# Interleaving the attention and mLSTM cores with the weight slabs of their projections

## The chip, the cores and the metric

The kernel runs on one core of one Trainium2 chip. The metric is device time in microseconds of one execution. The engines are called as in the profile: PE (TensorE, matmuls), PEld (its weight loads), DVE (VectorE), ACT (ScalarE), POOL (GpSimd), SP (the queue that issues the weight DMAs). Each engine works through its own list of instructions in order; between engines only semaphores order the work.

## What is computed

The reference runs two transformer blocks over 256 positions of width 1024: one with two FFNs and a gated delta mixer, then one with a differential attention layer, an MLP, an mLSTM layer and a second MLP. The change touches the attention and the mLSTM layer:

```
# attention: 8 heads, q and k of 2 x 64, v of 128
q, k, v = split(h @ w_in, 3)                   # w_in: 1024 x 3072
logits = q.k * 64**-0.5 + bias;  p = softmax(logits, causal)
attn = p[:, 0] - lam * p[:, 1]
o = rmsnorm(attn @ v, subln) * (1 - lambda_init);  out = o @ w_out
# mLSTM: 4 heads, q and k of 128, v of 256
q, k = silu(causal conv4((h @ w_in)[qk]));  v, o_pre = the next columns
Sc = (q.k) * exp(D - m);  num = Sc @ v;  den = sum(Sc)
h = num / max(|den|, exp(-m));  out = (sigmoid(o_pre) * rmsnorm(h)) @ w_out
```

## The kernel before

All activations are kept transposed (features on the partitions, 256 positions along the row). Every weight matrix is cut into slabs of 1024 x 256, and `Plan` lists the slabs in the order in which they are used. SP loads them into four `raw` buffers. To keep float32 accuracy with fast matmuls each slab is split into a high part `w_hi` and a low part `w_lo`, in two halves of four row tiles. ACT casts both halves (`split_hi`, L1021), DVE subtracts for half 0 (`ahead`, L1469) and POOL for half 1 (L549). There are four half buffers, so a half can be split once the half four places earlier has been multiplied. `half` on PE (L591) is 24 matmuls of 128x128 on 256 columns: high by high, high by low, low by high. On ACT and DVE, `ahead(n)` prepares slab n+1 while PE works on slab n.

A projection of w columns is a row of slabs into PSUM banks 0 and 1 in turn. When both halves of a slab are multiplied (`filled`), ACT evicts the bank (`evict`, L1087).

Attention (`attention`, one function for each engine) runs 12 slabs `aqkv` (four of q, four of k, four of v) one after another, then turns v by transposes (L880), and only then works off the heads: `scores` on PE (L891), bias, scaling and row maxima on DVE (L1924 to L1930), four exponentials on ACT (L1362), the combination of the two softmaxes on DVE (L1939 to L1947, signalled as `a_comb`), three transposes of it on PE (L904), a copy (L1371), the product with v on PE (L909 to L911) and a copy (L1373). After the last head one normalisation over all eight heads follows (L1951 to L1957), 16 transposes (L916), and the four slabs `ao` of the output projection.

mLSTM runs the gate matmuls (L926), four slabs `mqk` with a convolution on DVE (L1995, L1996) and a SiLU on ACT, eight slabs `mvo` (v and the output gate), and then four heads: row broadcasts and scores on PE (L950 to L953), exponentials on ACT (L1421), weighted scores on DVE (L2012), the products (L966 to L970), sums of squares (L974), root, reciprocal and scaling (L1432, L2027, L2028), gating (L2032) and the split of the result. Then the four slabs `mo`.

The order on each engine is written out by hand; nothing is planned at run time. On PE a wait holds back everything behind it.

## Time and profile before

| | us |
|---|---|
| median of 3 runs | 1689.58 (1689.15 to 1689.95) |
| profiled execution, its own time | 1690.33 |
| its span, first to last instruction | 1688.5 |
| PE busy | 1524.3 (90%) |
| DVE, ACT, POOL busy | 828.6, 690.7, 508.6 |
| mean granted TensorE clock | 0.948 of 2.4 GHz |

PE is busy 90% of the span, so the idle tenth and the stretches at the lower clock are what a reordering can reach. The shares are averages over stages; the two stages of the change lie from about 969 to 1120 us (attention) and from 1321 to 1484 us (mLSTM).

### The profile page before, as it was taken

Reading aid. Unit: us, or ns where it says so; the run is one execution under the profiler, and the core shown is the slowest. Engines: PE = TensorE matmul, PEld = TensorE weight load, DVE = VectorE, ACT = ScalarE, POOL = GpSimd, SP = SyncE. Lnnn points to the kernel's source line nnn. Section 1 sums busy time; section 2 is a strip of 40 time slices with the busy share of each in tenths; the row PEclk is TensorE's granted clock in tenths of the full one; section 3 lists DMA queues with packets and bytes.
Section 4 is the critical chain, followed back from the end, with each engine's and each line's share of the span. In section 5 each row is a group of like instructions: output and inputs, shape, how many; then the busy total and the mean of one; then the engine's idle time right before and its main releaser. Section 6 shows DMA issues by size and latency. Waiting matters only on the chain.

```text
span 1688.5 us, 30721 instructions
## 1 busy us (share of the span) xinstructions
PE 1524.3 (90%) x13577; PEld 1421.7 (84%) x13577; DVE 828.6 (49%) x1133; ACT 690.7 (41%) x961; POOL 508.6 (30%) x209
## 2 busy tenths in 40 slices
PE   5799999797987899899999898699999798899998
PEld 2699998686877787889999797589999597789997
DVE  0432335768676645673334533664433543754333
ACT  1343434543424442444444244535533355445432
POOL 0334432221112211334344242034444141234442
PEclk8899999898988999999999999699999898899999
DMA  9667683732212433336656363046565243245551
GB/s 325 172 219 256 197 277 118 256 104 72 77 51 76 153 123 127 125 125 225 225 169 203 115 200 125 1 137 188 175 200 175 72 154 101 73 127 187 189 185 39
DMA packets 236356, 258.31 MB, mean 153 GB/s; under 512 B 8442, under 2 KB 215744, under 8 KB 236224
## 3 DMA queue, kind: packets, MB, share of 16 engines
q1 hardware_dynamic: 229968, 252.13, 45.5%
q10 hardware_dynamic: 6255, 4.22, 1.3%
q8 instruction: 107, 1.75, 0.4%
q14 instruction: 26, 0.21, 0.0%
HBM read 253.71 MB, written 2.62 MB: 152 GB/s over the span
## 4 chain that ended last, share of the span: by engine, by line
PE 77%; DVE 12%; DMA 4%; ACT 4%; issue 3%; POOL 0%; SPq 0%; DVEq 0%; ACTq 0%
PE ps L591 63%; PE ps L799 4%; DMA bias_rows<-brow 2%; PE ps L565 2%; PE ps L615 2%; DVE w_lo L1469 1%; DVE uf L1501 1%; DVE rstd L1506 1%; DMA raw<-in_w_ada 1%; DVE mt L1604 1%; PE ps L574 1%; ACT w_hi L1021 1%; PE ps L863 1%; PE ps L849 1%; PE ps L926 1%
## 5 line engine op out<-in xcount | busy, mean ns | idle before, releaser
L591 PE MATMUL ps<-u_hl,w_hi 128*128 128x256 f32 x4544 | 849.2, 289 | 43.3 <-DVE w_lo L1469 16.6
L549 POOL TENSOR_TENSOR w_lo<-raw,w_hi 128x1024 fp32r<-128x1024 f32 (+1 forms) x204 | 508.1, 2492 | 1158.0 <-ACT w_hi L1021 1158.0
L591 PEld LDWEIGHTS ps<-u_hl,w_hi 128*128 128x128 f32 x4544 | 724.9, 196 | 66.8 <-issue 53.8
L591 PE MATMUL ps<-u_hl,w_lo 128*128 128x256 f32 x2272 | 651.0, 287 | 0.0
L1021 ACT CAST w_hi<-raw 128x1024 fp32r<-128x1024 f32 (+1 forms) x408 | 410.4, 1038 | 216.4 <-PE ps L591 198.3
L1469 DVE TENSOR_TENSOR w_lo<-raw,w_hi 128x1024 fp32r<-128x1024 f32 x204 | 310.0, 1522 | 317.8 <-ACT w_hi L1021 317.2
L591 PEld LDWEIGHTS ps<-u_hl,w_lo 128*128 128x128 f32 x2272 | 444.9, 196 | 0.0
L591 PE MATMUL ps<-mid_hi,w_hi 128*128 128x256 f32 x864 | 244.8, 283 | 0.0
L591 PE MATMUL ps<-mid_hi,w_lo 128*128 128x256 f32 x864 | 243.1, 281 | 0.0
L591 PE MATMUL ps<-mid_lo,w_hi 128*128 128x256 f32 x864 | 243.1, 281 | 0.0
L591 PEld LDWEIGHTS ps<-mid_hi,w_hi 128*128 128x128 f32 x864 | 162.7, 188 | 1.0 <-issue 0.8
L591 PEld LDWEIGHTS ps<-mid_lo,w_hi 128*128 128x128 f32 x864 | 162.7, 188 | 0.2
L591 PEld LDWEIGHTS ps<-mid_hi,w_lo 128*128 128x128 f32 x864 | 162.6, 188 | 0.0
L1885 DVE TENSOR_TENSOR mt<-sil 128x512 f32<-128x512 f32 x32 | 22.2, 693 | 92.6 <-ACT sil L1335 92.6
L565 PE MATMUL ps<-raw,cpad 128*32 128x512 f32 x288 | 40.2, 676 | 18.7 <-ACT cpad L1111 9.9
L1076 ACT CAST mid_hi<-mt 128x512 fp32r<-128x512 f32 x22 | 13.6, 619 | 96.8 <-DVE mt L1556 84.1
L1335 ACT ACTIVATE sil<-ps 128x512 f32<-128x512 f32 x32 | 19.2, 599 | 82.3 <-PE ps L591 82.3
L615 PE MATMUL ps<-uf,cst 128*128 128x256 f32 x144 | 40.3, 412 | 9.3 <-DVE uf L1484 9.3
L1556 DVE TENSOR_TENSOR mt<-sil,ps 128x512 f32<-128x512 f32 x22 | 15.1, 688 | 67.3 <-PE ps L591 67.3
L1534 DVE TENSOR_TENSOR hT<-hT,ps 128x512 f32<-128x512 f32 x16 | 11.0, 688 | 67.0 <-PE ps L591 67.0
L615 PEld LDWEIGHTS ps<-uf,cst 128*128 128x128 f32 x144 | 27.1, 204 | 17.6 <-DVE uf L1484 13.1
L1069 ACT ACTIVATE sil<-ps 128x512 f32<-128x512 f32 x22 | 13.2, 598 | 67.8 <-PE ps L591 67.8
(320 smaller groups left out, 1361.7 us busy)
## 6 DMA issues: line engine op xcount, KB each, us to landing
raw<-in_mlp_w SPq DMA_DIRECT2D x64, 1024.0 KB, 5.2
raw<-in_w_ffn_up SPq DMA_DIRECT2D x44, 1024.0 KB, 5.1
raw<-in_w_ada SPq DMA_DIRECT2D x36, 1024.0 KB, 5.5
raw<-in_w_in SPq DMA_DIRECT2D x30, 1024.0 KB, 5.1
raw<-in_w_ffn_down SPq DMA_DIRECT2D x16, 1024.0 KB, 6.0
raw<-in_attn_w_in SPq DMA_DIRECT2D x12, 1024.0 KB, 4.9
raw<-in_mlstm_w_in SPq DMA_DIRECT2D x12, 1024.0 KB, 5.1
raw<-in_w_ffn_down SPq DMA_DIRECT2D x8, 768.0 KB, 4.5
```

The lines of the kernel that those rows point to most:

```text
L549: pool.tensor_tensor(w_lo[half][:, 0:k, :], src, w_hi[half][:, 0:k, :].bitcast(F32), ALU.subtract).then_inc(low_ready(n, h)[0], 1)
L565: mm = pe.matmul(bank(b)[32 * k:32 * k + 32, :], cpad[:, 4 * a + k, :], raw4[r][:, k, :], start=(a == 0), stop=(a == 1), skip_group_check= ...
L574: mm = pe.matmul(bank(b)[:, q:q + 1], row_at(p)[:, q * P:(q + 1) * P], cs("ones")[:, 0:1], start=True, stop=True, skip_group_check=True)
L591: mm = pe.matmul(bank(b)[:, m * S:(m + 1) * S], a, c[:, k0 + kt, :], start=(first and m == 0 and kt == ks.start and q == 0), stop=(last an ...
L615: mm = pe.matmul(bank(2)[:, 0:S], cs("ones"), uf[:, k, :], start=(k == 0), stop=(k == KD - 1))
L799: mm = pe.matmul(bank(b)[rows, o:o + CH], left[rows, n, h, :], right(rows, n, h), start=True, stop=True)
L849: mm = pe.matmul(bank(4)[rows, h * P:(h + 1) * P], bmat[rows, n, h, :], rr[rows, h, :], start=True, stop=True)
L863: mm = pe.matmul(bank(5)[rows, h * P:(h + 1) * P], attm[rows, n, h, :], vn[rows, h, :], start=True, stop=True)
L1021: act.copy(w_hi[t % HALVES][:, 0:k, :], src).then_inc(hi_ready, 1)
L1335: act.activation(r, two(b), ACT.Relu).then_inc(bank_free[b], 1)
L1469: dve.tensor_tensor(w_lo[half][:, 0:k, :], src, w_hi[half][:, 0:k, :].bitcast(F32), sub)\
L1885: link(dve.tensor_tensor(m, r, r, mul))
```

## The change

The columns of q, k and v are no longer three blocks. The slabs come as q, k, v of heads 0 and 1, then of heads 2 and 3, and so on (four rounds j = 0 to 3 of three slabs, six halves called slots 0 to 5). During round j the heads 2j-2 and 2j-1 are worked off between the halves. The last two heads fall between the halves of the output projection, which is cut into two halves of its rows (heads 0 to 3, heads 4 to 7), with the normalisation in three parts (four, two and two heads). In mLSTM the q and k slabs come as 0, 2, 1, 3, and the four heads run between the halves of the eight `mvo` slabs. The first heads' results are kept in new buffers `x_hi`, `x_lo`, and several buffers of mLSTM are doubled. The matmuls of the projections and the work of each head stay as they were, but for small copies (`emb` on ACT) and smaller pieces of the normalisation.

```diff
-    columns("aqkv", A["attn_w_in_2"][0], 12)
-    columns("ao", A["attn_w_out_2"][0], 4)
+    for j in range(4):
+        for part in range(3):
+            plan.weight(("aqkv", 4 * part + j), A["attn_w_in_2"][0], 0, 8, (4 * part + j) * SLAB)
+            plan.group("aqkv", 4 * part + j)
+    for kh in range(2):
+        for c in range(2):
+            plan.weight(("ao", kh, c), A["attn_w_out_2"][0], 4 * kh, 4, 2 * c * SLAB, True)
...
+MQK = (0, 2, 1, 3)
@@ PE, attention @@
-                columns("aqkv", 12, U, u_ready("attn"))
...
-                for h in range(8):
-                    if h + 2 < 8:
-                        scores(h + 2)
                     pe.wait_ge(s("a_comb"), h + 1)
...
+                for j in range(4):
+                    for part in range(3):
+                        key = ("aqkv", 4 * part + j)
+                        b = open_bank(*key)
+                        for h in range(2):
+                            half(plan.slab[key], h, b, U, h == 0, h == 1, first if j == 0 and part == 0 else None)
+                            slot = 2 * part + h
+                            if j and slot == 1:
+                                v_columns(j - 1)
+                            if j and slot == 2:
+                                turn(2 * j - 2)
+                            if j and slot == 3:
+                                products(2 * j - 2)
+                                turn(2 * j - 1)
+                            if j and slot == 4:
+                                products(2 * j - 1)
+                            if j == 3 and slot == 4:
+                                pe.wait_ge(s("a_sread"), 5)
+                                features(0, 2)
+                                features(1, 3)
+                    scores(2 * j)
+                    scores(2 * j + 1)
...
+                pe.wait_ge(s("a_ready"), 2)
+                out_half(0, 0, X, every, True, False)
+                v_columns(3)
+                out_half(0, 1, X, every, True, False)
+                turn(6)
+                pe.wait_ge(s("a_sread"), 7)
+                out_half(0, 2, X, every, True, False)
+                products(6)
+                turn(7)
+                pe.wait_ge(s("a_sread"), 8)
+                features(2, 4)
+                out_half(0, 3, X, every, True, False)
+                products(7)
+                pe.wait_ge(s("a_ready"), 3)
+                for g in range(4):
+                    out_half(1, g, U, (0, 1), False, False)
+                    if g == 2:
+                        features(3, 5)
+                pe.wait_ge(s("a_ready"), 4)
+                for g in range(4):
+                    out_half(1, g, U, (2, 3), False, True)
+                    if g:
+                        squares("mlp0", g - 1)
+                squares("mlp0", 3)
@@ ACT, attention @@
+                for j in range(4):
+                    ahead(plan.slab[("aqkv", j)])
+                    if j == 3:
+                        root(0)
+                    if j:
+                        exps(2 * j - 2)
+                    take(0, j)
+                    ahead(plan.slab[("aqkv", 4 + j)])
+                    if j:
+                        v_columns(j - 1)
+                        exps(2 * j - 1)
+                        turned(2 * j - 2)
+                    take(1, j)
+                    ahead(plan.slab[("aqkv", 8 + j)])
+                    if j:
+                        outputs(2 * j - 2)
+                        turned(2 * j - 1)
+                        outputs(2 * j - 1)
...
+                    take(2, j)
@@ DVE, attention @@
+                for j in range(4):
+                    if j:
+                        scores(2 * j - 2)
+                    if j == 3:
+                        normed(0)
+                    ahead(plan.slab[("aqkv", j)])
...
+                    if j:
+                        scores(2 * j - 1)
+                    ahead(plan.slab[("aqkv", 4 + j)])
+                    if j:
+                        combined(2 * j - 2)
+                    ahead(plan.slab[("aqkv", 8 + j)])
+                    if j:
+                        combined(2 * j - 1)
+                    if j == 2:
+                        squared(0)
...
+                ahead(plan.slab[("ao", 1, 0)])
+                low(3, u_lo[:, 6:8, :], u_hi[:, 6:8, :])
+                ahead(plan.slab[("ao", 1, 1)])
+                for g in range(4):
+                    dve.wait_ge(halves_done, 2 * plan.slab[("ao", 1, g // 2)] + g % 2 + 1)
...
@@ PE, mLSTM @@
+                for j in range(8):
...
+                    half(n, 0, b, U, True, False)
+                    if j == 0:
+                        start_columns()
+                    if 1 <= j <= 4:
+                        v_columns(j - 1)
+                    if j in (2, 3):
+                        sums(j - 2)
+                    if j == 5:
+                        products(3)
+                    if j == 6:
+                        sums(3)
+                    half(n, 1, b, U, False, True)
+                    if j in (1, 2):
+                        products(j - 1)
+                    if j == 4:
+                        products(2)
+                    if j == 5:
+                        sums(2)
+                    if j < 4:
+                        scores(j)
@@ ACT, mLSTM @@
+                table(ACT.Silu)
...
+                    if j == 0:
+                        silu2(3)
+                        act.wait_ge(s("m_m"), 1)
+                        act.activation(rows2[:, 7, :], rows2[:, 7, :], ACT.Exp, scale=-1.0).then_inc(s("m_rows"), 1)
...
+                    if j == 7:
...
+                        act.activation(vo[:, 8:14, :], vo[:, 8:14, :], ACT.Sigmoid).then_inc(s("m_o"), 1)
+                        high(0)
+                        high(1)
@@ DVE, mLSTM @@
+                    if j == 4:
+                        scaled_out(0)
+                        scaled_out(1)
...
+                    if j == 7:
+                        dve.wait_ge(s("m_o"), 1)
+                        gated(0)
+                        gated(1)
+                        gated(2)
+                        low(0)
+                        low(1)
```

`take(part, j)` evicts a slab once both its halves are done; `turn(h)` is the three transposes (L904 of before), which wait for `a_comb`; `combined(h)` is the combination on DVE (L1939 to L1947 of before); `start_columns()` transposes the row behind `m_rows`.

## Rows read from the trace of the kernel before

**Rows 1.** The chain that ended last, attention: start us, us, what.
```profile
968.86 5.29 PE ps L591 x42
...
1087.56 3.68 PE ps L916 x16
...
1104.51 5.75 PE ps L591 x48
...
1118.39 1.14 PE ps L615 x4
```

**Rows 2.** Busy time by stretch, both cores: PE, PEld, DVE, ACT, POOL, clock, DMA, GB/s.
```profile
1038.40:1091.20 52.80, 31.27 (x169) 23.30 (x170) 37.02 (x85) 27.34 (x92) 0.00 (x0) 0.70 0.06 20
1411.50:1460.20 48.70, 37.71 (x136) 27.78 (x136) 25.42 (x44) 24.95 (x40) 0.00 (x0) 0.72 0.07 22
```

**Rows 3.** The chain, mLSTM: its first matmuls and the root behind its last.
```profile
1321.01 9.16 PE ps L926 x32
...
1484.32 0.48 ACT rms L1045
```

**Rows 4.** Timeline of PE: scores of one attention head at the full clock.
```profile
1067.62 0.93 PE L891 MATMUL ps<-qa 64*128 64x128 f32 x8
```

**Rows 5.** The chain: combination of head 0, from its start to the transposes.
```profile
1046.32 0.14 DVE stat L1939
...
1048.14 0.56 PE ps L904 x3
```

**Rows 6.** The chain, mLSTM: pieces of one head, from the row broadcast to the reciprocal.
```profile
1436.91 2.00 PE ps L950 x2
...
1444.37 0.38 ACT dn L1429
...
1445.30 1.14 PE ps L974 x4
...
1447.44 1.76 DVE rt L2027
```

**Rows 7.** Timeline of ACT and DVE in a steady slab.
```profile
1032.05 0.59 ACT L1087 COPY qa<-ps 128x512 f32<-128x512 f32 x1 [3.28 <-PE ps L591]
...
1032.54 2.00 ACT L1021 CAST w_hi<-raw 128x1024 fp32r<-128x1024 f32 x2
...
1033.62 1.23 DVE L1469 TENSOR_TENSOR w_lo<-raw,w_hi 128x1024 fp32r<-128x1024 f32 x1 [4.53 <-ACT w_hi L1021]
```

**Rows 8.** POOL beside DVE (timelines), and one line's instructions (min/median/max ns).
```profile
982.77 2.50 POOL L549 TENSOR_TENSOR w_lo<-raw,w_hi 128x1024 fp32r<-128x1024 f32 x1 [3.13 <-ACT w_hi L1021]
...
982.92 4.49 DVE L1913 TENSOR_TENSOR tz<-tz,cst 128x2048 f32<-128x2048 f32 x1
...
L1951 DVE TENSOR_TENSOR osq<-otm x1: 2293/2293/2293, 1079.9 to 1079.9; 128x2048 f32<-128x2048 f32 x1
```

**Rows 9.** Timelines: six steps of the convolution on DVE, beside POOL and without it.
```profile
1356.57 4.93 DVE L1996 SCALAR_TENSOR_TENSOR cac<-pad,prm,cac 128x256 f32<-128x256 f32 x6
...
1363.19 2.71 DVE L1996 SCALAR_TENSOR_TENSOR cac<-pad,prm,cac 128x256 f32<-128x256 f32 x6
```

**Rows 10.** Busy time by stretch around two stalls, columns as in rows 2.
```profile
1044.00:1048.00 4.00, 0.28 (x4) 0.00 (x0) 3.86 (x11) 3.50 (x15) 0.00 (x0) 1.00 0.00 0
1048.00:1052.00 4.00, 3.29 (x17) 2.60 (x17) 3.73 (x11) 1.76 (x7) 0.00 (x0) 0.60 0.00 0
...
1336.00:1340.00 4.00, 0.10 (x1) 0.00 (x0) 3.93 (x4) 2.48 (x3) 3.76 (x2) 0.86 0.01 2
1340.00:1344.00 4.00, 3.67 (x17) 3.70 (x18) 3.93 (x6) 0.00 (x0) 2.41 (x1) 0.50 0.69 201
1344.00:1348.00 4.00, 4.00 (x29) 4.00 (x28) 2.67 (x5) 0.00 (x0) 0.00 (x0) 0.78 0.24 67
```

**Rows 11.** Timeline of ACT: the table load ahead of the exponential.
```profile
1366.87 1.28 ACT L1408 ACT_TABLE_LOAD   x1
```

**Rows 12.** The page, part 6: weight loads of attention, KB each, us to landing.
```profile
raw<-in_attn_w_in SPq DMA_DIRECT2D x12, 1024.0 KB, 4.9
```

More of the change, by code:

```diff
@@ new lines, in out_banks, with out_half @@
+                def out_banks():
+                    return (open_bank("ao", 0), open_bank("ao", 1), 2, 3)
+                banks = out_banks()
+                def out_half(kh, g, hl, ks, first, last):
+                    n, h = plan.slab[("ao", kh, g // 2)], g % 2
+                    i = (2 * n + h) % HALVES
+                    hi, lo = hl
+                    sem, count = low_ready(n, h)
+                    pe.wait_ge(sem, count)
+                    for m in range(2):
+                        for kt in ks:
+                            x, y = (w[i][:, kt, m * P:(m + 1) * P] for w in (w_hi, w_lo))
+                            k = 4 * kh + kt if kh else kt
+                            for q, (a, c) in enumerate(((x, hi), (x, lo), (y, hi))):
+                                mm = pe.matmul(bank(banks[g])[:, m * S:(m + 1) * S], a, c[:, k, :],
+                                               start=(first and m == 0 and kt == ks[0] and q == 0),
+                                               stop=(last and kt == ks[-1] and q == 2), skip_group_check=True)
+                    if ks[-1] == 3:
+                        mm.then_inc(halves_done, 1)
@@ L928, in mlstm @@
                 mm.then_inc(s("m_gates"), 1)
-                columns("mqk", 4, U)
-                columns("mvo", 8, U)
-                pe.wait_ge(s("m_rows"), 1)
-                for t in range(2):
-                    mm = pe.transpose(bank(2)[:, 4 * t:4 * t + 4], rows2[0:4, 4, t * P:(t + 1) * P], cs("ident")[0:4, 0:4])
-                mm.then_inc(s("m_acol"), 1)
-                for j in (6, 7):
-                    b, before = plan.bank("mvo", j)
-                    pe.wait_ge(bank_free[b], before + 1)
@@ L938, in mlstm @@
[L938 to L950 removed]
+                for n in MQK:
+                    slab(("mqk", n), ("mqk", n), U)
@@ new lines, in start_columns, with scores @@
+                def start_columns():
+                    pe.wait_ge(s("m_rows"), 1)
+                    for t in range(2):
+                        mm = pe.transpose(bank(2)[:, 4 * t:4 * t + 4], rows2[0:4, 4, t * P:(t + 1) * P],
+                                          cs("ident")[0:4, 0:4])
+                    mm.then_inc(s("m_acol"), 1)
+                def scores(h):
+                    pe.wait_ge(s("m_qk"), (2, 2, 4, 4)[h])
+                    pe.wait_ge(s("m_acol_in"), 1)
+                    if h:
+                        pe.wait_ge(s("m_emb"), h)
+                        pe.wait_ge(s("m_v"), h)
+                    pe.matmul(bank(2), cs2("sel")[0:4, h * P:(h + 1) * P],
@@ L1435, in mlstm @@
+                high(2)
+                high(3)
                 table(ACT.Sqrt)
-                columns("mo", 4)
+                for j in range(4):
+                    ahead(plan.slab[("mo", j)])
             ffn("f1", "ffn1")
@@ L1930, in scores, with combined @@
                     dve.tensor_reduce(c[:, :, 1:2], x[:, :, 0:256], AX.X, ALU.max, negate=True).then_inc(s("a_max"), 1)
-                scores(0)
-                for h in range(8):
-                    if h < 7:
-                        scores(h + 1)
+                def combined(h):
                     dve.wait_ge(s("a_exp"), h + 1)
@@ new lines, in attention @@
+                low(0, x_lo[:, 0:2, :], x_hi[:, 0:2, :])
+                low(1, x_lo[:, 2:4, :], x_hi[:, 2:4, :])
+                scores(6)
+                squared(1)
+                scores(7)
+                ahead(plan.slab[("ao", 0, 0)])
+                combined(6)
+                combined(7)
+                normed(1)
+                ahead(plan.slab[("ao", 0, 1)])
+                low(2, u_lo[:, 4:6, :], u_hi[:, 4:6, :])
+                squared(2)
+                normed(2)
+                ahead(plan.slab[("ao", 1, 0)])
@@ new lines, in attention @@
+                low(3, u_lo[:, 6:8, :], u_hi[:, 6:8, :])
+                ahead(plan.slab[("ao", 1, 1)])
+                for g in range(4):
+                    dve.wait_ge(halves_done, 2 * plan.slab[("ao", 1, g // 2)] + g % 2 + 1)
+                    x = hT[:, 2 * g:2 * g + 2, :]
+                    b, before = plan.bank("ao", g) if g < 2 else (g, 0)
+                    op = dve.tensor_tensor(x, x, two(b), add)
+                    if g < 2:
+                        op.then_inc(bank_free[b], 1)
+                        dve.wait_ge(bank_free[b], before + 1)
+                    else:
+                        link(op)
+                    square(g)
```

393 lines of the change are left out of this document (236 added, 157 removed).

## The prediction

> **What bounds the kernel now.** I read the page, then the chain of waits in order, then busy time and clock by stretch in the two stages. In the projections PE never stops: a slab of 48 matmuls takes 5.75 us [rows 1], 2.88 a half. The two cores are different. In 52.8 us of attention's core PE is busy 31.3, at a mean clock of 0.70; in 48.7 us of mLSTM's it is 37.7 at 0.72 [rows 2]. There PE waits for DVE and ACT, and POOL, whose weight work has run out, shows 0.00. The whole stages, to the end of their last squares, last 968.9 to 1119.5, 150.7 us [rows 1], and 1321.0 to 1484.3, 163.3 us [rows 3]. The rest of the program is not touched.
>
> **What can be gained.** In the new order only PE's work of the cores must remain. Busy time times clock is 31.3 x 0.70 = 22 us for attention [rows 2]. Of it a head's scores take 0.93 at the full clock [rows 4] and its transposes 0.56 [rows 5]; the 16 transposes of a set take 3.68 at half clock [rows 1], 1.84 at full, and there are two sets. That leaves (22 - 11.9 - 3.7) / 8 = 0.8 for a head's products. In a stream some latency overlaps, so I take 20.5. An mLSTM head takes 7.4 us at half clock up to its moments (1436.9 to 1444.4), so 3.7, and 0.9 of sums [rows 6]; with the v transposes four heads are 20.3 (27 by [rows 2], whose busy time holds latencies). If nothing else came up, 32 and 28 us would go, 60 in all.
>
> **What the change adds: waits in PE's order.** Take a round j = 1 to 3 of attention. PE can transpose head 2j-2 only after `combined(2j-2)`. On DVE that stands behind `ahead` of the k slab, the subtraction for half 0 of the v slab. That needs ACT's cast, and on ACT the cast stands behind `take(0, j)`, the eviction of the q slab, which waits for the end of slot 1. From there: eviction 0.6, one cast 1.0, subtraction 1.23 [rows 7], combination 1.8 [rows 5]; 4.7 with the handovers.
>
> A fifth term comes from POOL. When DVE's subtraction ends, ACT's second cast (1.0 after the first) is already there, so POOL starts its 2.5 us on half 1. In [rows 8] the same thing happens: POOL starts at 982.77, the DVE instruction behind its own subtraction takes 4.49 us, and another of that shape takes 2.29 while POOL is idle. In [rows 9] six steps of the convolution take 4.93 with a POOL instruction among them and 2.71 without. The combination's instructions read two SBUF tensors or are of the kind of one-tensor instruction that waited too, so I add 2.3 us: 7.0 from the end of slot 1. PE has the v transposes (0.46) and slot 2 (2.88) meanwhile and waits 3.7 us.
>
> The Trainium skill (SBUF — State Buffer, "Who interferes with whom") has the rule for this: of DVE and GpSimd, whoever issues first gets the shared pair of ports for the whole instruction and the other fully blocks. It speaks against this change, which moves the combination from beside an idle POOL to beside a working one. By that rule the trace agrees (4.49 against 2.29); without it the sum would be that of rival A.
>
> The second head is worse. `combined(2j-1)` stands behind the subtraction for the next q slab, and its cast behind `take(1, j)`, which waits for the end of slot 3. The same 7.0 us pass, and PE, whose `turn(2j-1)` comes directly after slot 3, has only `products(2j-2)`, 0.8 us: it waits 6.2 us with slots 4 and 5 queued behind it, though their weights are ready. A round waits 9.9 us, three rounds 29.7.
>
> In the output projection I count four waits by the same addition: 3.3 for `turn(6)`, behind `squared(1)`, `scores(7)` and a subtraction; 4.0 for the fourth `ao` slab, whose subtraction stands behind the last normalisation; 4.3 for the first squares, whose residual stands behind a cast that needs a half freed by the second pass (1.0 + 1.2 + POOL 2.4 + 0.7 + 0.7, less half an `out_half`, and the port once more); and 1.0 for the last squares, as now. Sum 12.6.
>
> **The clock.** After a PE gap of 3.9 us (1044.3 to 1048.1) the granted clock fell to half, 1.2 GHz, and after one of 4.2 us (1336.1 to 1340.3) PE worked 3.67 us at 0.50 and then some 1.8 more [rows 10]: 2.7 us lost. Every round has two gaps of this size. No row shows one of 6 us in a stream of halves; the price lies between nothing and the 14 us at half clock (7 us lost) that followed the gap of 1044. I take 2.7, the nearest row, for each of six, and 4 for the tail: 20 us.
>
> Attention: 16 slabs 92.2, core 20.5, squares 1.8, waits 29.7 + 12.6, clock 20: 176.8 us against 150.7, **26 us more**.
>
> **mLSTM.** The four `mqk` slabs keep their order of convolution and their waits (7.5 us now; I take the same; the earlier SiLU table, 1.28 us [rows 11], lies behind DVE's gate rows, and costs 1.5 if that cover is gone). Then: `start_columns` after the first half of `mvo` waits for `m_rows`: from the last `mqk` slab eviction 0.6, convolution 3.3 (up to 2.2 more beside POOL, [rows 9]), SiLU 0.9, table 1.28 [rows 11], exponential 0.4, against one half and the wait before it: 5.6. The heads wait for ACT and DVE: 1.6 and 2.1 for the first two sums (Square before them is behind two casts and the exponentials), 3.5 for `products(2)`, which needs head 0's bank and so `scaled_out(0)`, behind a table load, a root and a reciprocal of 1.76 [rows 6], and 0.6 elsewhere: 7.8. At the end `mo` waits for the sigmoid, three gatings and `low(0)` on DVE beside POOL: 6.4. With gates 9.2, slabs 92.2, core 20.3, squares 1.8 + 1.0 and clock 7: 158.8 against 163.3, **4 less**.
>
> **Edits without a price.** Loads come in another order but have the same size, land in 4.9 us [rows 12] and are issued four slabs (23 us) ahead; were that cover gone, each of 28 slabs could cost its share of 4.9. SP waits for nothing new. DVE's and ACT's total work hardly changes; per round they have 22 us of PE time for some 11 and 14 us.
>
> **Sum.** 1690.33 + 26 - 4 = 1712.3 for an execution like the profiled one, and that lies 0.75 above the median, so 1711.6.
>
> **The rivals.**
> (A) *POOL and DVE hardly meet in the rounds*, because POOL comes in after the combination. Then the waits are 1.4 and 3.9 in place of 3.7 and 6.2, 5.3 a round, 16 in three; only one gap a round costs clock (8), and the tail is 6 with 2 of clock: 114.5 + 16 + 8 + 8 = 146.5, 4 less than now; mLSTM, with 2.3 less at three of its waits and a spell less of the low clock, 10 less. 1690.3 - 4 - 10 = 1676: faster. It decides once a handover costs under about half a microsecond. For: small shifts decide who is first. Against: in every slab POOL's half is ready 0.2 us before DVE's subtraction ends [rows 7].
> (B) *The clock holds* through the gaps. Then 156.8 and 151.8 us stand against 150.7 and 163.3: 1690.3 + 6 - 11.5 = 1685. Against: both gaps of 4 us in [rows 10] lost it.
> (C) *The clock stays low through the rounds*, as in the present core after one gap. Of a round's 22 us of PE work some 16 run at half in place of 5: 11 more a round less what is in the 20 already, so 8 a round and 1735.
>
> **How the numbers follow.** Forecast 0.73, its own range 1699 to 1722 (clock 10 to 28 us, tail and mLSTM each 4 off). A 0.13, B 0.08, C 0.06. About 0.2%, 3.4 us, is what a measurement of this kernel can tell from no change: faster is A and most of B, 0.19; same, between B and the forecast, 0.04; slower 0.77. The range 1684 to 1724 leaves out A and C.
>
> **What would show it.** In the changed kernel PE waits for DVE's combination six times, 3.7 and 6.2 us in turn, with clock 0.5 behind them; DVE's small combination instructions are over 2 us where POOL is busy; one long PE wait for `m_rows` and one ahead of `mo`. Waits of 1 and 4 us at a full clock, or none, would make it A. Halves of 2.88 us right behind the gaps would make it B.

## The result and the profile after

The changed kernel takes 1711.7 us (median of 4 runs, 1711.5 to 1712.7), the kernel before 1689.4 on the same chip: a ratio of 1.0134, 95% interval 1.012 to 1.0148. The change makes the kernel 22.3 us slower. Forecast were 1711.6 and slower. The profiled execution has a span of 1709.8 us at a mean clock of 0.947; before it was 1688.5 at 0.948.

The totals tell little: PE is busy for 1525.8 us in place of 1524.3, and the rest of the loss is time in which PE stands still. So the stages come first. The point at which [rows 1] begin is this one in the timeline of PE (start us, us, engine, line, operation; in brackets the idle time before it):

```profile
969.98 0.51 PE L604 MATMUL ps<-u_hl,w_hi 128*128 128x256 f32 x2 [0.36 <-DVE u_hl L1725]
```

And these are, in the chain of waits (start us, us, what), the root behind attention's last squares, the first gate matmul of mLSTM and the root behind its last squares, as in [rows 3].

```profile
1146.91 0.48 ACT rms L1171
```

```profile
1348.35 1.87 PE ps L1019 x4
...
1505.39 0.48 ACT rms L1171
```

Attention lasts 176.9 us (969.98 to 1146.9) against 150.7: 26.2 more. mLSTM lasts 157.0 against 163.3: 6.3 less. Together that is 19.9; 1.1 more had been lost ahead of attention, in stages that the change leaves alone (969.98 against 968.86), and the spans differ by 21.3.

**Where attention's time goes.** What PE waited for from 960 to 1180 us (engine and line waiting, what for; us in total, times, the longest):

```profile
PE ps L921 <- DVE aa L2145: 30.3, 7, 5.8
PE ps L628 <- DVE uf L1692: 4.9, 3, 4.1
PE ps L983 <- DVE w_lo L1677: 3.6, 1, 3.6
...
PE ps L604 <- DVE w_lo L1677: 2.8, 1, 2.8
```

L921 is `turn`, L2145 the end of `combined`. The seven waits are 3.2, 5.8, 3.2, 5.8, 3.2, 5.8 in the three rounds (27.0) and 3.3 for head 6. L983 is the fourth half of `ao`, L628 the squares, and the 2.8 under L604 stand in round 0. The chain through round 1 shows how one wait comes about (start us, us, what):

```profile
1006.28 4.20 PE ps L604 x24
...
1010.50 0.02 ACT qa L1213
...
1010.98 1.06 ACT w_hi L1147
...
1012.06 1.23 DVE w_lo L1677
...
1013.41 2.11 DVE stat L2138
...
1015.55 0.56 DVE a1t L2142 x2
...
1016.93 0.90 PE ps L921 x3
```

PE ends slot 3, ACT evicts the k slab, and only then casts; DVE subtracts, and only then combines; PE goes on 6.4 us after the end of its half. One of these steps is out of proportion. L2138 scales two numbers per partition. Here is its neighbourhood in the timeline:

```profile
1013.05 2.43 POOL L562 TENSOR_TENSOR w_lo<-raw,w_hi 128x1024 fp32r<-128x1024 f32 x1 [8.97 <-ACT w_hi L1147]
1013.21 0.17 DVE L2137 RECIPROCAL stat<-stat 128x4 f32<-128x4 f32 x1
1013.41 2.10 DVE L2138 TENSOR_SCALAR stat<-stat,lam 128x2 f32<-128x2 f32 x1
```

It ends when POOL's subtraction ends. The reciprocal ahead of it is not held up. All instructions of the line in the stage (min/median/max ns) show that it is 2.1 us beside POOL and 0.23 alone:

```profile
L2138 DVE TENSOR_SCALAR stat<-stat,lam x8: 228/2099/2120, 1002.0 to 1108.1; 128x2 f32<-128x2 f32 x8
```

Behind the wait the clock is at half. Columns as in [rows 2]: stretch, PE, PEld, DVE, ACT, POOL, clock, DMA, GB/s.

```profile
1010.80:1016.60 5.80, 0.33 (x3) 0.14 (x2) 4.43 (x7) 2.45 (x4) 2.43 (x1) 0.95 0.00 0
1016.60:1020.00 3.40, 3.07 (x15) 3.07 (x16) 0.28 (x1) 0.48 (x1) 0.00 (x0) 0.50 0.96 305
1020.00:1023.00 3.00, 3.00 (x16) 3.00 (x16) 0.00 (x0) 0.00 (x0) 0.00 (x0) 0.53 0.03 9
1023.00:1026.00 3.00, 3.00 (x28) 3.00 (x27) 0.00 (x0) 0.37 (x1) 0.00 (x0) 1.00 0.00 0
```

PE stands still for 5.8 us, then works at 1.2 GHz (16 matmuls in 3 us, against 28 at the full 2.4). Summed over the stretches at half clock, PE works 42.8 us of the stage in them, so 21.4 us are lost; 27.1 of the 42.8 lie in the three rounds, 12.3 behind them and 3.4 in round 0.

**Where mLSTM gains.** What PE waited for from 1340 to 1520 us:

```profile
PE ps L604 <- DVE x_hl L2302: 5.3, 1, 5.3
PE ps L1028 <- ACT rows L1617: 4.9, 1, 4.9
PE ps L604 <- DVE w_lo L1677: 4.8, 4, 2.3
...
PE ps L1069 <- ACT nsq L1600: 3.2, 2, 1.8
PE ps L1059 <- DVE uf L2287: 3.1, 1, 3.1
```

In this order: the wait ahead of `mo`, `m_rows`, the `mqk` slabs, the sums of heads 0 and 1, the products of head 2. With 0.6 at the squares it is 21.9 us, and PE works 18.6 us at half clock, where before it was 38.0 in this stage. The `mqk` slabs had 7.5 us of waits before. Most of the difference is one step of the gate rows on DVE, ahead of the subtraction for the first slab. In the chain of the kernel before (first line) it stands beside POOL, in that of the changed kernel it does not, and POOL falls on the convolution behind it:

```profile
1336.34 2.27 DVE rows L1982
```

```profile
1364.33 0.29 DVE rows L2239
...
1366.76 5.03 DVE cac L2253 x2
```

PE's wait ahead of this slab went from 4.2 to 2.25 us; the one behind the convolution is 1.1.

### The profile page after: what moved, and what is told of

Its sections match the earlier page's. It is cut to its first block, busy times and chain, and to the rows that moved or that the text cites. A ratio compares the mean times of both kernels' runs of the same rounds, so it can differ in the third digit from the quotient of the medians.

```text
span 1709.8 us, 30773 instructions
## 1 busy us (share of the span) xinstructions
PE 1525.8 (89%) x13577; PEld 1428.9 (84%) x13577; DVE 850.4 (50%) x1141; ACT 688.8 (40%) x966; POOL 506.5 (30%) x209
## 3 DMA queue, kind: packets, MB, share of 16 engines
q8 instruction: 107, 1.75, 0.4%
## 4 chain that ended last, share of the span: by engine, by line
PE 74%; DVE 15%; DMA 4%; ACT 4%; issue 3%; SPq 0%; POOL 0%; DVEq 0%; ACTq 0%
PE ps L604 59%; PE ps L812 4%; DMA bias_rows<-brow 2%; PE ps L578 2%; DVE w_lo L1677 2%; PE ps L628 2%; ACT w_hi L1147 1%; DVE cac L2253 1%; DVE uf L1709 1%; PE ps L983 1%; DMA raw<-in_w_ada 1%; DVE rstd L1714 1%; DVE stat L2138 1%; DVE mt L1812 1%; PE ps L587 1%
## 5 line engine op out<-in xcount | busy, mean ns | idle before, releaser
L604 PE MATMUL ps<-u_hl,w_hi 128*128 128x256 f32 x4352 | 828.1, 292 | 39.9 <-DVE w_lo L1677 16.2
L604 PEld LDWEIGHTS ps<-u_hl,w_hi 128*128 128x128 f32 x4352 | 703.9, 199 | 64.1 <-issue 51.9
L604 PE MATMUL ps<-u_hl,w_lo 128*128 128x256 f32 x2176 | 628.8, 289 | 0.0
L604 PEld LDWEIGHTS ps<-u_hl,w_lo 128*128 128x128 f32 x2176 | 431.8, 198 | 0.0
L604 PE MATMUL ps<-mid_hi,w_hi 128*128 128x256 f32 x864 | 244.8, 283 | 0.0
L604 PE MATMUL ps<-mid_hi,w_lo 128*128 128x256 f32 x864 | 243.1, 281 | 0.0
L604 PE MATMUL ps<-mid_lo,w_hi 128*128 128x256 f32 x864 | 243.1, 281 | 0.0
L604 PEld LDWEIGHTS ps<-mid_hi,w_hi 128*128 128x128 f32 x864 | 162.7, 188 | 1.0 <-issue 0.8
L604 PEld LDWEIGHTS ps<-mid_lo,w_hi 128*128 128x128 f32 x864 | 162.7, 188 | 0.2
L604 PEld LDWEIGHTS ps<-mid_hi,w_lo 128*128 128x128 f32 x864 | 162.6, 188 | 0.0
L578 PE MATMUL ps<-raw,cpad 128*32 128x512 f32 x288 | 39.8, 670 | 18.7 <-ACT cpad L1237 9.8
L628 PE MATMUL ps<-uf,cst 128*128 128x256 f32 x144 | 42.5, 429 | 13.3 <-DVE uf L1692 13.3
L1202 ACT CAST mid_hi<-mt 128x512 fp32r<-128x512 f32 x22 | 13.6, 619 | 96.4 <-DVE mt L1764 84.3
L628 PEld LDWEIGHTS ps<-uf,cst 128*128 128x128 f32 x144 | 28.5, 215 | 22.3 <-DVE uf L1692 17.3
```

The costliest lines, as they stand in the source:

```text
L578: mm = pe.matmul(bank(b)[32 * k:32 * k + 32, :], cpad[:, 4 * a + k, :], raw4[r][:, k, :], start=(a == 0), stop=(a == 1), skip_group_check= ...
L604: mm = pe.matmul(bank(b)[:, m * S:(m + 1) * S], a, c[:, k0 + kt, :], start=(first and m == 0 and kt == ks.start and q == 0), stop=(last an ...
L628: mm = pe.matmul(bank(SQ_BANK.get(norm, 2))[:, 0:S], cs("ones"), uf[:, k, :], start=(k == 0), stop=(k == KD - 1))
```

## The experiments

Eleven kernels were run, in three sessions; each is compared with runs of the kernel before in its own session (1689.6 us for the first four below, 1691.3 for the order of the tail, of mLSTM and for the last version, 1690.9 for the others). Where a run is set against the changed kernel, that is its 1711.7, from a session with 1689.4. The output is computed in full in all of them. Except for the filling of PE, two waits of POOL, and a sigmoid split in two and a table load in the kernels that say so, they only change where something stands. My theory was the prediction's: PE's waits come from the order of the small steps on ACT and DVE, POOL makes each longer, and the clock comes on top. The rivals are named run by run. The 95% interval of a run's ratio is 0.12 to 0.2% to either side, 2 to 3 us, so smaller differences between runs decide nothing.

**One stage at a time.**

```diff
 # attention only: mlstm() of PE, ACT and DVE, its buffers and its slab order as before
-MQK = (0, 2, 1, 3)
+MQK = (0, 1, 2, 3)
```

> Attention as changed, mLSTM as in the kernel before (its functions, its buffers and its order of slabs). My account: the stages are independent, and in the traces the mLSTM stage went from 163.3 us before to 157.0 after, so without its part the kernel is 6.3 us above the changed one: 1718.0, 28.6 above the kernel before, with PE's six waits for the combination unchanged (3.2 and 5.8 in turn). The forecast's own term (4.5 us for mLSTM) would give 1716.2. Rival: the part in mLSTM only looks like a gain in its own stage and is paid back around it (at the first slabs behind it): then 1711.7, no difference.

Measured: 1718.2 us, ratio 1.0169 (1.015 to 1.0189).

The other way round, attention() and its slabs are those of before and mLSTM is changed:

> mLSTM as changed, attention as in the kernel before. My account: 1689.4 - 6.3 = 1683.1, a little faster than the kernel before (ratio 0.9963), with the waits of the changed kernel in this stage: 4.9 for m_rows, 1.5 and 1.8 for the sums, 3.1 for the products of head 2, 5.3 for the output projection. Rival, as for the run above: 1689.4 within 0.2%. A sum of the two runs' differences that is not the whole difference of 22.3 us would mean that the stages act on one another.

Measured: 1683.6 us, ratio 0.9959 (0.9945 to 0.9974). Its waits are those of the changed kernel, to within 0.1 us. The two differences, +28.6 and -6.0, add up to 22.6, against 22.3 for both: within some 3 us the stages do not act on one another, and the part in mLSTM alone makes the kernel faster.

**POOL's share of a wait.**

```diff
                     pool.wait_ge(hi_ready, 2 * n + h + 1)
+                    if h == 1 and n in HELD:
+                        pool.wait_ge(s("a_comb"), HELD[n])
```

`HELD` gives the v slab of round j the value 2j-1, and the next slab 2j.

> The changed kernel, but POOL may subtract half 1 of a v slab only after the combination of head 2j-2, and half 1 of the next slab only after that of head 2j-1 (j = 1 to 3); nothing else differs, and PE needs these halves only slots later. It takes away the overlap of POOL and DVE at the combination and nothing else. My account (DVE's one-tensor and two-tensor steps stand still while POOL's subtraction of 2.5 us runs): the second small step of a combination goes from 2.1 us to 0.23, PE's waits from 3.2 and 5.8 to 1.2 and 3.8, and the three short gaps no longer cost clock: 6 x 2.0 + 3 x 1.7 to 3.4 = 17 to 22 less, 1690 to 1695. Rival 1, POOL is not the cause and the small step waits for something else (ACT's exponentials, a semaphore's latency): waits and time as in the changed kernel, 1711.7. Rival 2, POOL's own half is late then: a new PE wait on POOL's half in slot 5 or slot 1, of 1 us or more.

Measured: 1695.8 us, ratio 1.0034 (1.002 to 1.0048), so 15.9 less than the changed kernel, just under the 17 to 22 expected. The same line of the combination, and what PE waited for:

```profile
L2143 DVE TENSOR_SCALAR stat<-stat,lam x8: 228/228/229, 1001.9 to 1090.2; 128x2 f32<-128x2 f32 x8
```

```profile
PE ps L926 <- DVE aa L2150: 19.0, 7, 3.9
PE ps L633 <- DVE uf L1697: 4.7, 2, 4.1
PE ps L988 <- DVE w_lo L1682: 3.6, 1, 3.6
```

The six waits are 1.3 and 3.9 in turn: 15.7 in place of 27.0, 1.9 less each, which is what L2138 lost beside POOL. No new wait appears. That POOL is the cause is shown: nothing but the time of its subtraction was moved. The Trainium skill (SBUF — State Buffer, "Who interferes with whom") gives the shared pair of ports to whoever issues first and names `tensor_scalar` among the operations that can take it; by that rule, the trace agrees (2.1 us beside POOL, 0.23 without). Behind the gaps of 1.3 us the clock stayed at full, and the work at half clock in the rounds fell from 27.1 to 12.3 us: 11.3 of waiting and 7.4 of clock make 18.7; the part from the start of the stage to `turn(6)` is shorter by 18.1 in the profiled executions, and the medians show 15.9.

**The clock's share.**

```diff
                 def turn(h):
-                    pe.wait_ge(s("a_comb"), h + 1)
                     if h:
                         pe.wait_ge(s("a_aT"), h)
+                    if h < 6:
+                        for _ in range((3, 6)[h % 2]):
+                            pe.matmul(bank(6), cs("ident"), cst[:, 0:512], start=True, stop=True, skip_group_check=True)
+                    pe.wait_ge(s("a_comb"), h + 1)
```

> The changed kernel with idle matmuls on PE (128x512, into a bank that is free in this stage, results unused), three ahead of the wait for the combination of an even head, six ahead of that of an odd head, heads 0 to 5. They fill part of a gap that PE spends waiting anyway, so the handovers stay and only the clock is tested. My account: the granted clock falls because PE stands still. Behind the six gaps of the changed kernel 34.0 us are worked at half clock (3.4, 6.8, 3.4, 6.8, 6.8, 6.8), 17 us lost; with the gaps filled they go: 1711.7 - 17 = 1695, less up to 3 if the rest of a gap still costs a spell, so 1695 to 1698. Rival: these spells are not caused by the gaps (or by the chip's state, or by the slabs), and the filling changes nothing: 1711.7 or a little above.

Measured: 1699.7 us, ratio 1.0057 (1.0042 to 1.0071), 12.0 less. The handovers, from the end of a half to the transposes that wait for the combination, are what they were: from the end of slot 3 in round 1 to `turn(1)` 6.46 us pass, 6.45 in the changed kernel. The filling takes 2.7 and 5.3 us of a gap and leaves 0.6 to 0.7. And through the rounds the clock is full:

```profile
1000.00:1091.40 91.40, 87.55 (x592) 70.80 (x591) 52.27 (x76) 43.11 (x96) 21.95 (x9) 1.00 0.29 95
```

In the changed kernel it is 0.84 from 1000 to 1104.7. So the six gaps cost 12 us by the clock, besides the 27 for which they last. My expectation of 17 counted the whole stretches at half clock (34.0 us); PE works in 27.1 of them, which makes 13.6, and of that some lies in the small products inside a handover, where PE waits anyway.

The price of the same gaps is also not the same in each execution. In the profiled executions of other kernels whose six waits are those of the changed one (3.2 and 5.8 us in turn), PE works 20.1 us at half clock in the rounds with attention alone changed, 20.2 with the tail's order, 22.0 with the bias late and 27.7 with the order of mLSTM alone: 10 to 14 us lost for the same gaps, 13.6 in the changed kernel. With the bias late the second gap of 3.2 us, the one ahead of 1032.32, cost nothing:

```profile
1029.10:1032.30 3.20, 0.04 (x1) 0.00 (x0) 3.09 (x5) 1.49 (x8) 1.77 (x1) 1.00 0.28 28
1032.30:1036.40 4.10, 4.08 (x33) 3.90 (x33) 0.00 (x0) 1.10 (x3) 0.00 (x0) 1.00 0.65 246
```

**Which link of the order makes the wait.** First DVE:

```diff
+                    if j:
+                        combined(2 * j - 2)
                     ahead(plan.slab[("aqkv", 4 + j)])
                     if j:
-                        combined(2 * j - 2)
-                    ahead(plan.slab[("aqkv", 8 + j)])
-                    if j:
                         combined(2 * j - 1)
+                    ahead(plan.slab[("aqkv", 8 + j)])
```

> The changed kernel, but on DVE the combination of head 2j-2 stands ahead of the subtraction for the v slab, and that of head 2j-1 ahead of the subtraction for the next q slab (j = 1 to 3). No instruction is added or taken away. My account: both waits of a round come from this order alone (the combination stands behind a subtraction, that behind a cast, the cast behind an eviction that waits for the end of a slab); the exponentials are there before. All six waits of PE go to 1 us or less (27.0 us, so 23 to 27 saved) and with them most of the 26.5 us worked at half clock in the rounds (13 lost): 1711.7 - 36 = 1676, 1674 to 1682. Rival 1, POOL's lock finds the combination wherever it stands: then waits of 1 to 2 us remain at each turn and the time is 1684 to 1690. Rival 2, the subtractions become late in their place, and PE waits for the weight halves instead (for half 0 of the v slab and of the q slab, up to 3 us each): 1690 to 1700.

Measured: 1672.9 us, ratio 0.9902 (0.9883 to 0.9921): 38.8 less than the changed kernel, 1 us below the 1674 to 1682 expected, and faster than the kernel before. In the chain of round 1 nothing but PE is left:

```profile
998.42 2.88 PE ps L604 x24
1001.30 0.33 PE ps L921 x3
1001.62 2.87 PE ps L604 x24
...
1005.16 0.53 PE ps L921 x3
1005.70 2.88 PE ps L604 x24
```

```profile
1000.00:1066.20 66.20, 63.96 (x541) 61.71 (x540) 43.41 (x71) 42.91 (x96) 23.20 (x9) 1.00 0.41 133
```

Of the 27.0 us of waits 2.2 are left, in round 3, and the lost clock is back: 24.8 + 12 to 13.6, together 37 to 38. The rival of the late subtractions falls: no PE wait for a half of weights is new. That of POOL's lock falls in five handovers of six. In the sixth it is what is left; the last step of the combination starts 0.11 us behind POOL and takes 2.80 us for its two instructions, 0.75 in the other handovers:

```profile
1043.74 2.36 POOL L562 TENSOR_TENSOR w_lo<-raw,w_hi 128x1024 fp32r<-128x1024 f32 x1 [5.06 <-ACT w_hi L1147]
1043.85 2.80 DVE L2145 SCALAR_TENSOR_TENSOR aa<-sc,stat,a1t 128x128 f32<-128x128 f32 x2
```

Then ACT, with DVE's order left alone:

```diff
-                    take(0, j)
                     ahead(plan.slab[("aqkv", 4 + j)])
+                    take(0, j)
...
-                    take(1, j)
                     ahead(plan.slab[("aqkv", 8 + j)])
+                    take(1, j)
```

> The changed kernel, but on ACT the two casts ahead stand before the eviction of the q slab and before that of the k slab, in every round; DVE's order is left alone, so the combination still stands behind the subtraction. It tests the link that the forecast puts first: the cast waits for the end of slots 1 and 3 only since it stands behind the eviction. The half buffer that the first cast needs is free a slot earlier. My account: the subtraction and the combination of head 2j-2 run before the end of slot 1, PE's 3.2 us waits vanish; the second head's exponentials stand behind the eviction and the second cast, so the 5.8 us wait shrinks, to 0 to 2 us: 1711.7 - 21 to 27 - 10 to 13 of clock, 1672 to 1681. Rival 1, the subtraction was late for another reason (its load, or POOL): no change, 1711.7. Rival 2, the second cast, which does need the end of the slot, now delays the eviction and with it exponentials and scores: the 5.8 us waits stay and only the first of each round go: 1711.7 - 9.6 - 4 = 1698.

Measured: 1684.2 us, ratio 0.9965 (0.9953 to 0.9977): 27.5 less, but 3 us above the 1672 to 1681 that I expected. The six waits fall from 27.0 to 9.4. The 3.2 us waits did not vanish, as I had it, but are 2.1, 2.1 and 3.2; the 5.8 us waits are 1.0, about nothing and 1.0. And the wait of round 0 grows from 2.85 to 4.8: POOL, earlier by this order, starts at 982.96, just ahead of the subtraction that PE needs (983.20), where in the changed kernel it came behind it. What is left in round 1 is POOL again, which now starts earlier too:

```profile
1003.22 1.22 DVE L1677 TENSOR_TENSOR w_lo<-raw,w_hi 128x1024 fp32r<-128x1024 f32 x1
1003.88 2.81 POOL L562 TENSOR_TENSOR w_lo<-raw,w_hi 128x1024 fp32r<-128x1024 f32 x1 [3.63 <-ACT w_hi L1147]
...
1004.56 2.15 DVE L2138 TENSOR_SCALAR stat<-stat,lam 128x2 f32<-128x2 f32 x1
```

That the cast stands behind the eviction is one link; that the combination stands behind the subtraction is the other. Breaking either takes most of the wait away, the second more of it.

**The wait I had not foreseen.**

```diff
                     ahead(plan.slab[("aqkv", j)])
-                    if j == 0:
-                        dve.wait_ge(s("tz_in"), 16)
...
                     ahead(plan.slab[("aqkv", 8 + j)])
                     if j:
                         combined(2 * j - 1)
+                    if j == 0:
+                        dve.wait_ge(s("tz_in"), 16)
...
```

> The changed kernel, but DVE's two steps that prepare the attention bias (4.5 to 5 us together, and the wait for their transfer) stand at the end of round 0 instead of behind its first subtraction. It tests the 2.85 us wait of PE in round 0, which the forecast did not have. My account: in the changed order these steps stand ahead of the subtraction for the v slab of round 0 and hold it up; moved, the wait goes, and with it the 3.4 us at half clock behind it: 1711.7 - 2.85 - 1.7 = 1707.1. Rival: the v slab of round 0 waits for its load or its cast, so the gap stays: 1711.7.

Measured: 1707.0 us, ratio 1.0093 (1.0073 to 1.0112), 4.8 less, as expected, though the interval is some 3 us to either side; its trace shows that the gap of round 0 is gone. In the changed kernel the steps stand there, behind their transfer and ahead of the subtractions (timeline of DVE):

```profile
973.93 1.23 DVE L1677 TENSOR_TENSOR w_lo<-raw,w_hi 128x1024 fp32r<-128x1024 f32 x1 [0.47 <-ACT w_hi L1147]
977.65 2.29 DVE L2180 TENSOR_TENSOR tz<-tz,cst 128x2048 f32<-128x2048 f32 x1 [2.50 <-DMA tz<-bias_rows]
979.98 2.75 DVE L2182 COPY tz<-tz 128x1024 f32<-128x1024 f32 x1
982.76 4.57 DVE L1677 TENSOR_TENSOR w_lo<-raw,w_hi 128x1024 fp32r<-128x1024 f32 x2
```

**The tail alone.** On DVE the sums of squares (`squared(1)`) go behind `combined(6)`, `ahead` for the last half ahead of `squared(2)` and `normed(2)`, and the last `ahead` behind the first residual and its squares; ACT casts that half ahead of `outputs(7)`.

```diff
                 scores(6)
-                squared(1)
                 scores(7)
-                ahead(plan.slab[("ao", 0, 0)])
                 combined(6)
+                ahead(plan.slab[("ao", 0, 0)])
+                squared(1)
                 combined(7)
...
+                ahead(plan.slab[("ao", 1, 0)])
                 squared(2)
                 normed(2)
-                ahead(plan.slab[("ao", 1, 0)])
```

> The changed kernel with the order of attention's output projection alone altered: on DVE the sums of heads 4 and 5 behind the combination of head 6, the subtraction for the last half slab ahead of the last normalisation, the first residual and squares ahead of the last subtraction; on ACT the cast for that half ahead of the last output copy. My account of the tail (waits of 3.3 for head 6, 3.6 for the fourth half, 4.1 for the first squares, 0.6 for the last, and 10.2 to 13.6 us at half clock behind them): the three waits become 0.7, 1.1 and 1.5, so 7.7 less, and 4 to 5 of clock: 1711.7 - 12 = 1700. Rival, these waits are ends of longer chains (products, roots, loads) and reappear one step later: within 3 us of 1711.7.

Measured: 1695.6 us, ratio 1.0033 (1.002 to 1.0046), 16.1 less, 4 more than expected. The waits of 3.3, 3.6 and 4.1 became 0, 1.1 and 1.5. They were not ends of longer chains. I had too little for the clock: in the changed kernel PE works 12.3 us at half clock from the gap ahead of `turn(6)` to the last squares, here the clock is full up to there, and 3.4 us at half follow behind them. The waits (8.4) and that clock (6.1) make the 14.5 us by which the profiled executions differ.

**mLSTM alone.** On PE `start_columns` goes behind half 1 of the first `mvo` slab, `sums(0)`, `sums(1)` and `products(2)` each half a slab later; the sigmoid of the first four of the six rows, and with it `gated(0)` and `gated(1)`, do not wait for the other two; `gated(2)` goes behind `low(0)` and `low(1)`.

```diff
-                        act.activation(vo[:, 8:14, :], vo[:, 8:14, :], ACT.Sigmoid).then_inc(s("m_o"), 1)
+                        x = vo[:, (8, 12)[j - 6]:(12, 14)[j - 6], :]
+                        act.activation(x, x, ACT.Sigmoid).then_inc(s("m_o"), 1)
```

> The changed kernel with the order in mLSTM alone altered (columns, sums of heads 0 and 1, products of head 2 each half a slab later on PE; sigmoid and gating of heads 0 and 1 one slab earlier). In the run with all orders altered the waits of 4.85, 1.45, 1.75, 3.1 and 5.3 us became 2.0, 0, 0, 0 and 4.6, with 0.35 for the columns; so 9.4 less, and of clock about 1: 1711.7 - 10.5 = 1701. Rival, in that run part of this came from the attention's side (another clock at the start of the stage): 1704 to 1706.

Measured: 1702.9 us, ratio 1.0071 (1.0051 to 1.0091), 8.9 less. That lies between my 1701 and the rival's 1704 to 1706, and the interval takes in both; the waits below speak for my account, as attention is that of the changed kernel here. The waits are 2.1 with 0.35 for the columns in place of 4.85, nothing in place of 1.45 and 1.75, 0.2 in place of 3.1, and 4.6 in place of 5.3.

**All of it together.** DVE's combinations first, the bias late, the tail and mLSTM as above, in one kernel.

> The changed kernel with every wait of PE that its trace shows taken up by order alone. Attention: both combinations first, as in the run above, and the bias late; in the tail the normalisation's sums behind the combination, the cast and the subtraction for the last half ahead of the last normalisation, the first residual ahead of the last subtraction. mLSTM on PE: the columns transposed behind half 1 of the first slab, the sums of heads 0 and 1 half a slab later, the products of head 2 half a slab later; on ACT and DVE the sigmoid and gating of heads 0 and 1 one slab earlier. My account: rounds -36, bias -4.5, tail 3.3 + 3.6 + 4.1 down to about 1.5, -9.5 and -4 of clock; mLSTM 4.85 + 1.45 + 1.75 + 3.1 + 5.3 down to about 4, -12.5 and -5 of clock: 1711.7 - 71 = 1640, 1635 to 1655: faster than both kernels. Rival, PE's waits have a second chain close behind the first (ACT's or DVE's load, POOL's lock), so that half or more comes back: 1665 to 1680.

Measured: 1646.0 us, ratio 0.9737 (0.9722 to 0.9751), inside my range and far from the rival. Attention has gaps of 2.2, 1.1 and 1.5 us left, and PE works there 3.4 us at half clock, in place of 42.8.

The last version takes up four of the waits still seen: attention's first root goes to the end of round 2 and its normalisation behind `combined(4)`; the cast and the subtraction for the second `mqk` slab ahead of the gate rows; the exponential of the rows ahead of the last SiLU, with one table load more; `moments(3)` and `sums(3)` beside those of head 2, and the gating of heads 0 and 1 a slab earlier.

> The kernel with all orders altered (1646.0 us), with four of the waits that its trace still shows taken up: the first root and normalisation of attention behind the combination of their round (2.2 us); in mLSTM the first cast and subtraction ahead of the gate rows (2.25), the exponential of the rows ahead of the last SiLU (2.0), and the moments and sums of head 3 with those of head 2, so that the gating ends a slab earlier (4.6). My account: each of these waits goes or falls below 1 us, 10 less, and 3 to 5 of clock: 1646 - 14 = 1632. Rival, the last wait of mLSTM is bound by the gating of the last head and by POOL's lock on it, and stays over 3 us, and the tables loaded anew (one SiLU and one square root more) cost what the rows gain: 1638 to 1642.

Measured: 1635.9 us, ratio 0.968 (0.966 to 0.9699), 10 less than the run before it: between my account and the rival. The waits for the gate rows and for `m_rows` (2.25 and 2.0) became 0 and 1.1, but 1.9 instead of 1.1 stands at a `mqk` slab; that in round 3 is still 1.8, since the normalisation now holds up the next subtraction, and takes 3.4 us beside POOL, where in the run before it took 1.7. And the last wait of mLSTM is 4.6 as before. Its chain:

```profile
1387.05 2.64 DVE dn L2285
...
1391.85 1.67 DVE rt L2294
...
1394.23 1.67 DVE rt L2294
...
1396.53 3.75 DVE uf L2302 x4
...
1402.17 1.83 PE ps L604 x7
```

It stays over 3 us, as the rival said, but it is not the gating alone: from 1387 on DVE works without a pause, on the scaling of heads 2 and 3, whose result nobody needs yet, and the gating of heads 0 and 1 stands behind it. Two of the steps are lengthened by POOL (2.64 for an instruction that takes 0.42 at the second head, 3.75 for four instructions of gating, two of which take 0.87 right after). That the scaling of heads 2 and 3 could go behind it wasn't tried.

## Why the prediction was right

The mechanism was right, and the closeness is luck. The total fell within 0.1 us of the forecast, while the kernel before alone moves by 1.9 us from session to session (1689.4 to 1691.3). The terms were each off by more: round 0, missed, cost 4.5 us, the waits of the rounds and the tail were 3.7 less, mLSTM gained 1.8 more, and 1.1 was lost ahead of attention, for which the forecast had nothing.

- **Attention's rounds.** The mechanism is the one forecast, link by link, and the runs with DVE's and ACT's order altered confirm both links. The waits were 3.2 and 5.8, not 3.7 and 6.2: 27.0 against 29.7. The term that was off is POOL's: I added 2.3 us, and L2138 loses 1.9, because POOL starts about 0.3 us before it.
- **The tail.** 3.3, 3.6, 4.1 and 0.6, in sum 11.6, against 12.6. Right in place and size.
- **Round 0 was missed.** The prediction adds up the moves of the heads' steps, and left out one other move: the steps on the bias began at 982.9 in the kernel before [rows 8] and no wait of PE followed; they stand at 977.7 in the changed one, behind a wait for their transfer (it lands 6.9 us after 970.75) and ahead of two subtractions that PE needs at once. It cost 2.85 us and 1.7 of clock; 4.8 by the run, 3 to either side.
- **The clock.** 20 forecast, 21.4 measured, by other parts than I gave: 13.6 for the six gaps (16.2 forecast, so 2.3 each and not 2.7; 2.0 by the run with the filling, and from 1.7 to 2.3 in the executions of other kernels with the same gaps), 6.1 for the tail (4), 1.7 for round 0 (0). Between nothing and 7 for a gap, the stall of 4.2 us in [rows 10] was the right row to go by.
- **PE's own work in the core.** 176.9 less 92.2 for slabs, 1.8 of squares, 41.5 of waits and 21.4 of clock leaves 20.0, against 20.5.
- **mLSTM.** 6.3 less, where 4.5 was forecast (158.8 against 163.3). The waits were 21.9, not 28.3: each was over by a tenth to two fifths, and the `mqk` slabs, for which I took over the 7.5 us of before, had 4.8. By the traces, 2.0 of this 2.7 went with POOL's lock on the gate row, shown above; no run moves that lock alone. I had taken this part to be the same, since its order is. Against it stand 2 us more of clock (9.3 against 7) and some 2.3 us more of PE's own work than the 20.3 that I took; the larger of the two figures in the prediction (27, from the busy time) was too large, the smaller one too small.
- **The rivals.** A gave waits of 1.4 and 3.9 if POOL and DVE did not meet. With POOL held back the waits were 1.3 and 3.9: A's mechanism was priced rightly for the waits, and it did not happen, because POOL's half was ready just ahead of L2138 in all six handovers. Its total (1676) was too low: with POOL out of the way in the rounds the kernel takes 1695.8, since A also took 6.6 of waits and 2 of clock from the tail and nearly 4 us more from mLSTM than it gained, neither of which came with POOL out of the way in the rounds, and counted nothing for round 0. B, the clock that holds, would be the run with filled gaps: but for the tail and mLSTM it is what 12 us less looks like. It did not happen at any gap of 2.85 us or more in attention in the profiled execution of the changed kernel; with the bias late it did at one of the six. C did not happen: at the latest 5.9 us behind the end of a gap the clock was full again (1074.91 to 1080.85). Its price was also summed wrongly: 16 us of work at half in place of 5 are 11 us more a round, and these 5 are what the 20 us of clock hold; taking it off once more, to 8, gave 1735, where the sum is some 1745.

What the prediction did not ask is whether the order inside a round was needed. Most of the waits that it listed were ones of order, and the floor of 60 us below the kernel before, worked out in its second part, was nearer than its forecast suggested: 55 of it was reached in the last version (1691.3 to 1635.9 in its session).

## What to carry to other kernels

When small steps of one chain are dealt out between the halves of another, look on every helping engine for what stands ahead of them and what that waits for. A step whose inputs have long been there must not stand behind one that waits for PE, and two places in a list decided 39 us here. Price a PE gap like those here (3 to 6 us) at its length plus some 2 us for the half clock behind it, as a mean: a gap of 3.2 us cost nothing in two executions and 3.0 in another; where the gap can't be closed, idle matmuls buy the second part back. And when two engines share a port, ask what stands on one at the moment in which the other's work becomes ready: here it fell on the same instruction in all six handovers of the three rounds, and when the order changed it moved to another.

## What was unexpected about the hardware

- A DVE step on two numbers per partition took 2.1 us beside POOL's subtraction and 0.23 without it. The reciprocal directly ahead of it began 0.16 us after POOL and was untouched (0.17). Where it was held up, it ended within 0.05 us of POOL's instruction, however small the DVE step was.
- Idle matmuls of 128x512 inside a wait, with 0.6 to 0.7 us of silence left, kept the clock at full in six cases of six. In attention's rounds no gap of up to 1.3 us was followed by half clock in any run, but behind attention one was: in the kernel with the tail's order changed the gap of 1.32 us ahead of 1136.36 was followed by 3.4 us at half, and the same gap in the others was not. Each gap of 3.3 us or more in attention was followed by half clock. Between them it went both ways: after two gaps of 2.1 us in one kernel (the one with the cast first) the clock fell once, after gaps of 2.24 us it fell in one kernel (all orders together) and stayed full in another (DVE's combinations first), and after one of 3.2 us it stayed full in two kernels, while it fell behind all three in the changed one. What decides there stays open.
- The same order of instructions can pass POOL's lock on to another step, as in the gate rows. So slabs whose own steps keep their order lost 2.7 us of waiting (7.5 to 4.8), 2.0 of it at that step.
